# A two-layer hybrid decoder trunk on one core: twelve convolution taps of the second mixer go from TensorE to VectorE, and the first unit, the gate chain and the score levels are reordered

## The reference

```python
def token_mixer(h, ...):                       # h = rmsnorm(x): 256 x 1024
    z = h @ w_in                               # q, k 256 each; v, g 512; gr 16; ca, cb 512
    log_a = log_sigmoid(gr @ w_gate_up + b_gate) / 16
    o = gla_chunked(q / 8, k, v, log_a)        # 4 heads, gated linear attention, causal
    o = rmsnorm(o) * silu(g)
    u = ca * sigmoid(cb)                       # 512 channels
    u = causal_dwconv(u, conv_w, conv_b)       # 31 taps, each channel by itself
    u = silu(layernorm(u))                     # over the 512 channels
    return concat([o, u]) @ w_out

# layer 0: x + swiglu(h), width 2816.  layer 1: x + top-2-of-8 experts of the same width
```

## Time and profile before

| | us |
|---|---|
| median of three runs | 1210.74 |
| the profiled execution | 1210.83 |
| its span | 1209.0 |
| TensorE (PE) matmul busy | 1193.7 (99%) |
| VectorE (DVE) busy | 981.4 (81%) |
| ScalarE (ACT) busy | 795.6 (66%) |
| GpSimd (POOL) busy | 48.9 (4%) |

### The profile page before, as it was taken

How to read it: one execution, slowest core, us unless ns; L and a number is a source line. 1 busy time by engine, 2 the same in 40 slices (tenths; PEclk the granted TensorE clock), 3 DMA queues, 4 the chain that set the end, 5 groups by cost and what they waited for, 6 DMA issues and landing times.

```text
span 1209.0 us, 16770 instructions
## 1 busy us (share of the span) xinstructions
PE 1193.7 (99%) x6775; PEld 1030.6 (85%) x6775; DVE 981.4 (81%) x938; ACT 795.6 (66%) x757; POOL 48.9 (4%) x77
## 2 busy tenths in 40 slices
PE   8999999999999999999999999999999999999997
PEld 8998999999899888888888888888888888888885
DVE  5998664445669879989979879879889979979987
ACT  5976544334567657687768768668668668767764
POOL 4000000000100000000000000000000000000000
PEclk9999999999999999999999999999999999999999
DMA  9942555655545159999999999999999999999990
GB/s 273 369 139 86 192 175 178 197 183 179 204 160 190 54 189 368 380 370 392 375 374 391 376 375 389 377 376 388 381 385 375 381 386 373 381 388 375 395 341 36
DMA packets 182556, 359.61 MB, mean 297 GB/s; under 512 B 9190, under 2 KB 68940, under 8 KB 182476
## 3 DMA queue, kind: packets, MB, share of 16 engines
q1 hardware_dynamic: 178284, 343.28, 79.3%
q0 software_dynamic: 4176, 15.21, 3.3%
q10 hardware_dynamic: 16, 0.00, 0.0%
HBM read 350.60 MB, written 7.86 MB: 296 GB/s over the span
## 4 chain that ended last, share of the span: by engine, by line
PE 89%; DVE 5%; ACT 2%; issue 1%; SPq 1%; DMA 1%; ACTq 0%; DVEq 0%
PE YB L2018 18%; PE WBS L1997 13%; PE WBS L1999 13%; PE WBS L1998 13%; PE YB L1635 6%; PE WBS L1562 4%; PE WBS L1564 4%; PE WBS L1563 4%; PE YB L2009 2%; PE YB L2033 2%; PE WBS L1749 1%; DVE acc L1013 1%; PE YB L1616 1%; DVE w_lo L916 1%; DMA raw<-in_w_in 1%
## 5 line engine op out<-in xcount | busy, mean ns | idle before, releaser
L916 DVE TENSOR_TENSOR w_lo<-raw,w_hi 128x2048 fp32r<-128x2048 f32 x319 | 716.1, 2285 | 86.1 <-ACT w_hi L571 85.9
L571 ACT ACTIVATE w_hi<-raw 128x2048 fp32r<-128x2048 f32 x324 | 598.9, 1915 | 14.2 <-DMA raw<-in_w_in 10.2
L1997 PE MATMUL WBS<-w_hi,t_hi 128*128 128x512 f32 x704 | 278.7, 396 | 0.6 <-DVE w_lo L916 0.5
L1999 PE MATMUL WBS<-w_hi,t_lo 128*128 128x512 f32 x704 | 274.8, 390 | 0.0
L1998 PE MATMUL WBS<-w_lo,t_hi 128*128 128x512 f32 x704 | 274.3, 390 | 0.0
L1997 PEld LDWEIGHTS WBS<-w_hi,t_hi 128*128 128x128 f32 x704 | 132.3, 188 | 29.8 <-issue 2.9
L1999 PEld LDWEIGHTS WBS<-w_hi,t_lo 128*128 128x128 f32 x704 | 132.1, 188 | 28.2
L1998 PEld LDWEIGHTS WBS<-w_lo,t_hi 128*128 128x128 f32 x704 | 132.4, 188 | 26.3
L1562 PE MATMUL WBS<-t_hi,w_lo 128*128 128x256 f32 x448 | 127.5, 285 | 0.0
L1563 PE MATMUL WBS<-t_hi,w_hi 128*128 128x256 f32 x448 | 126.8, 283 | 0.0
L1564 PE MATMUL WBS<-t_lo,w_hi 128*128 128x256 f32 x448 | 126.8, 283 | 0.0
(11 more groups left out here) (315 smaller groups left out, 1384.3 us busy)
## 6 DMA issues: line engine op xcount, KB each, us to landing
raw<-in_we_down SPq DMA_DIRECT2D x88, 1024.0 KB, 7.0
raw<-in_we_gate SPq DMA_DIRECT2D x80, 1024.0 KB, 7.0
raw<-in_we_up SPq DMA_DIRECT2D x80, 1024.0 KB, 6.9
raw<-in_w_in SPq DMA_DIRECT2D x20, 1024.0 KB, 5.7
raw<-in_wd_gate SPq DMA_DIRECT2D x11, 1024.0 KB, 5.3
raw<-in_wd_up SPq DMA_DIRECT2D x11, 1024.0 KB, 5.4
raw<-in_wd_down SPq DMA_DIRECT2D x11, 1024.0 KB, 4.9
raw<-in_w_out SPq DMA_DIRECT2D x8, 1024.0 KB, 8.1
```

The source lines that it names most:

```text
L571: act.activation(w_hi[:, hi_slot(n, item), :], raw[slot][:], ACT.Copy).then_inc(hi_ready, 1)
L916: dve.tensor_tensor(w_lo[slot][:], raw[slot][:], w_hi[:, hi_slot(n, item), :].bitcast(F32), ALU.subtract).then_inc(lo_ready, 1)
L1997: pe.matmul(bank, xs_hi[:, k0 + k, :], hi[:, k, :], start=start, stop=False)
L1999: ins = pe.matmul(bank, xs_lo[:, k0 + k, :], hi[:, k, :], start=False, stop=stop)
```

## The change

It has four parts.

1. **First unit in halves.** SP loads the first unit of V0 as two transfers, and ScalarE and VectorE make its first half before they split the first token tile's activations. GpSimd's cast of the masks waits for the third unit's `w_hi`.
2. **Gate chain moved up**, in the first mixer alone: ScalarE does Abs, Exp and Ln ahead of units 3, 4 and 5, and VectorE's `cum` comes ahead of their `w_lo`.
3. **Levels in pairs.** TensorE does levels 0 and 1 one behind the other, and levels 2 and 3. The read-out of level 3 goes from ScalarE's eight block copies to one masked copy on VectorE. This holds for both mixers.
4. **Twelve taps.** In the second mixer the last six items of group 2 (taps 25 to 30 and, with them, 9 to 14) go from TensorE to VectorE. TensorE then has 26 items; between the levels stand 2, 2, 1, 1 and 4. VectorE's second batch of diagonal matrices has two in place of eight. VectorE adds its share to TensorE's (two new instructions), and ScalarE's copy of the second half waits for the first of these.

```diff
@@ constants @@
-        COARSE, FINE = 4, 5
-        COARSE_READS = [2, 4, 8, 16]
+        COARSE, FINE = 3, 6
+        COARSE_READS = [2, 4, 8]
+        SHARED = 6
+        PE_WORK = [PE_CONV, PE_CONV[:len(PE_CONV) - SHARED]]
+        DVE_WORK = [DVE_CONV, DVE_CONV[:42] + [(2, w) for n in range(TAPS - SHARED, TAPS) for w in (n - APART, n)] + DVE_CONV[42:]]
+        FIRST_SHARED = TAPS - SHARED - APART
@@ sync @@
+                if n == 0:
+                    dst = raw[0][:].rearrange("p (k c) -> p k c", k=k)
+                    sp.dma_start(dst[:, 0:k // 2], src[:, 0:k // 2]).then_inc(first_half_raw, 16)
+                    sp.dma_start(dst[:, k // 2:], src[:, k // 2:]).then_inc(raw_ready[0], 16)
+                    return
@@ gpsimd @@
+            pool.wait_ge(hi_ready, 3)
             step(pool.tensor_copy(masks[:], mask_f[:]))
@@ scalar, mixer @@
-                hi(b + 4)
-                hi(b + 5)
+                if l:
+                    hi(b + 4)
+                    hi(b + 5)
                 preload(ACT.Exp)
...
                 act.activation(Difs[:, 0], Difs[:, 0], ACT.Ln, bias=1.0).then_inc(gate_ln, 1)
-                hi(b + 6)
+                if l:
+                    hi(b + 6)
+                else:
+                    hi(b + 3)
+                    hi(b + 4)
+                    hi(b + 5)
...
-                coarse(3)
                 diagonals(3)
                 decays(7)
                 diagonals(7)
...
-                    for c in (2, 3):
+                    if l and r:
+                        act.wait_ge(shares_added, 1)
+                    for c in ((3,) if l else (2, 3)):
@@ scalar, start @@
             square(0, 1)
+            act.wait_ge(first_half_raw, 16)
+            act.activation(w_hi[:, hi_slot(0), 0:UNIT // 2], raw[0][:, 0:UNIT // 2], ACT.Copy).then_inc(first_half_hi, 1)
             turned(0, 0)
...
-            hi(3)
             mixer(0)
@@ vector, mixer @@
+                        if c == 2:
+                            if w == FIRST_SHARED:
+                                dve.wait_ge(cu_ready, 2 * l + 2)
+                                dve.tensor_scalar(acc[:, c, :], cu[:, c, w:w + T], ...).then_inc(conv_step[c], 1)
+                            else:
+                                dve.wait_ge(conv_step[c], shared_taps.index(w))
+                                dve.scalar_tensor_tensor(out=acc[:, c, :], ...).then_inc(conv_step[c], 1)
...
-                conv(8)
+                if l:
+                    conv(24)
+                else:
+                    lo(b + 5)
+                    conv(12)
+                    lo(b + 6)
...
-                conv(18)
+                conv(14)
...
-                conv(8)
+                level_read_out(3)
+                conv(6)
...
+                if l:
+                    dve.wait_ge(conv_step[2], 2 * SHARED)
+                    for r in (1, 0):
+                        rows = slice(64 * r, 64 * (r + 1))
+                        if r == 0:
+                            dve.wait_ge(conv_placed, 4 * l + 1)
+                        dve.tensor_tensor(acc[rows, 2, :], acc[rows, 2, :], WB[2 + r][rows, 0:T], ALU.add).then_inc(shares_added, 1)
+                    dve.wait_ge(shares_added, 2)
@@ tensor, mixer @@
                 level(0)
+                level(1)
                 pe.wait_ge(cu_ready, 2 * l + 1)
                 channels("CA1")
-                level(1)
                 channels("CB1")
-                level(2)
                 pe.wait_ge(v_ready, 2 * l + 1)
                 tokens("G0")
+                level(2)
                 level(3)
...
-                conv(3)
+                between = [2, 2, 1, 1, 4] if l else [3, 3, 3, 3, 4]
+                conv(between[0])
                 level(5)
```

More of the change, by code:

```diff
@@ L265, in trunk @@
         diag_ready, diag_used = sem("diag_ready"), sem("diag_used")
-        conv_step = [sem(f"conv_step{c}") for c in range(2)]
+        conv_step = [sem(f"conv_step{c}") for c in range(3)]
+        shares_added = sem("shares_added")
         pairs_ready, batch_ready, conv_done, conv_placed, conv_added, acc_summed = (sem(s) for s in (
@@ L683, in mixer @@
                 decays(1)
+                if l == 0:
+                    hi(b + 6)
                 hi(b + 7)
@@ L1081, in mixer @@
                 dve.tensor_copy(gr_t, YB[0:2 * RANK, 0, 0:T]).then_inc(gr_copied, 1)
-                if l == 0:
-                    lo(b + 2)
-                    lo(b + 3)
-                    lo(b + 4)
-                lo(b + 5)
+                lo(b + 5 if l else b + 2)
                 dve.wait_ge(logit_done, l + 1)
@@ L1103, in mixer @@
                 ins.then_inc(cum_ready, 1)
+                if l == 0:
+                    lo(b + 3)
                 differences(0)
                 differences(1)
-                lo(b + 6)
+                lo(b + 6 if l else b + 4)
                 conv_input(0)
                 make_pairs()
-                conv(8)
+                if l:
[4 more added lines that the diff above has]
+                    lo(b + 6)
                 decayed(0)
@@ L1211, in _ @@
             normalize(0, 1)
-            turned(0, 0)
             for half, made, ready in ((0, first_half_hi, first_half_lo), (1, hi_ready, lo_ready)):
+                if half:
+                    turned(0, 0)
                 part = slice(UNIT // 2 * half, UNIT // 2 * (half + 1))
@@ L1736, in conv @@
                 def conv(count):
-                    for c, w in PE_CONV[done[0]:done[0] + count]:
+                    for c, w in PE_WORK[l][done[0]:done[0] + count]:
                         n = done[0]
@@ L1749, in conv @@
                             ins = pe.matmul(WB[2 + r][:, T * (c - 2):T * (c - 1)], both[rows, :], cu[rows, c, w:w + T],
[L1750 removed]
+                                            start=(w == APART - 1), stop=(w == TAPS - 1 or n == len(PE_WORK[l]) - 1))
                         if n < BY_SCALAR:
                             ins.then_inc(diag_used, 1)
[L1753 removed]
+                        elif n == len(PE_WORK[l]) - 1:
                             ins.then_inc(conv_done, 1)
@@ L1835, in mixer @@
                 pe.wait_ge(v_ready, 2 * (l + 1))
-                conv(3)
+                between = [2, 2, 1, 1, 4] if l else [3, 3, 3, 3, 4]
+                conv(between[0])
                 level(5)
-                conv(3)
+                conv(between[1])
                 level(6)
-                conv(3)
+                conv(between[2])
                 level(7)
-                conv(3)
+                conv(between[3])
                 level(8)
-                conv(4)
+                conv(between[4])
                 pe.wait_ge(coarse_read, COARSE_READS[-1] * (l + 1))
```

26 lines of the change are left out of this document (15 added, 11 removed).

## The result

| | before | after |
|---|---|---|
| median of 20 runs each, us | 1210.77 (1210.29 to 1211.2) | 1212.58 (1210.47 to 1214.28) |
| ratio, 95% interval | | 1.0016, 1.0010 to 1.0022 |
| profiled execution, us | 1210.83 | 1212.21 |
| its span, us | 1209.0 | 1210.4 |
| TensorE busy, VectorE busy, us | 1193.7, 981.4 | 1191.5, 987.2 |

The change made the kernel slower by 0.16%, 1.8 us. I had forecast 1210.6 and no change. The time lies in the range given, but the direction is not the one forecast. I had taken 2.4 us for the least that a measurement can tell from no change; with 20 runs of each kernel the interval is 0.7 us to either side, and the 1.8 us stand clear of it. The runs after also lie further apart: 3.8 us, against 0.9 us before.

A forecast was written before the change was run, and what follows sets the result against it. The prediction took TensorE's work plus a few short waits as the bound. First mixer -1.8, second mixer -0.8, +1.9 and +0.6 summed to -0.1: 1210.6 us against the median, no change, range 1208.3 to 1212.6.

The forecast's parts named there:

- The start: First token tile: with the first unit in halves, TensorE's fifth k-step starts at 12.9 instead of 13.98; gain 1.0 us.
- The gate chain up: First mixer: moving it gives nothing by itself and costs nothing; unit 3 (Q) keeps 0.4 us of slack.
- The sum: First mixer as a whole: 1.0 from the start plus 0.8 from the pairs, 1.8 us gained.
- Levels in pairs: Both mixers: each pair saves one set of rounded/plain float32 switches, 0.39 us; two pairs gain 0.8 us a mixer.
- Twelve taps, up to level 4: Second mixer: shared taps in a row stand 0.5 us apart; VectorE meets level 4, 0.8 us earlier, just in time.
- From level 4 to o: Second mixer: TensorE waits for silu behind the sixteenth diagonal matrix; o starts 13.75 us after level 4, not 11.85, 1.9 later.
- Behind o: Second mixer, o to output projection: the same matmuls stand there, with the same 12 and 4 items; no cost counted.
- a late unit 3: First mixer, rival: unit 3 behind the gate chain comes late, 1212.2 us with a slip of 2.0, 1213.2 with 3.0; chance 0.10.
- The layernorm: Second mixer: VectorE's extra taps and additions make centring late, so TensorE waits 0.6 us before the squares' sum.
- Silu not last: Second mixer, rival: o waits for VectorE's last copy, 12.3 us after level 4 in place of 13.75; 1209.2 us; chance 0.22.
- the halves did bring their gain: Start of the kernel, rival denied here: the halves bring nothing, 0 in place of 1.0, so 1211.6 us; chance 0.13.

The follow-up runs named there:

- experiment 8: The kernel before with the first unit in halves alone; cast and gate chain stay: 1210.65 us, ratio 0.9998.
- Experiments 8 to 10: On the kernel before: halves alone (experiment 8), paired levels alone (1210.49 us), halves and paired levels together (1210.58 us).
- Experiment 3: The changed kernel with twelve unread 128x128 matmuls on TensorE in the wait before o of the second mixer: 1211.06 us, ratio 1.0004.
- experiment 6: The kernel of experiment 2 with the first half of unit 12's `w_lo` behind VectorE's centring in the second mixer: 1210.14 us, ratio 0.9993.
- experiment 2: The changed kernel with silu ahead of the last six diagonal matrices in the second mixer: 1209.43 us, ratio 0.9995.
- experiment 4: The changed kernel with six unread matmuls on TensorE in the wait before o of the second mixer: 1211.86 us, ratio 1.0006.
- experiment 5: The changed kernel with 3, 3, 3, 3 and 4 items between the second mixer's levels and six fewer behind o: 1209.17 us, ratio 0.9987.

## Why the prediction was wrong

**The start** was −1.0 and measured −1.44. The mechanism was right; VectorE began 0.29 sooner than the 9.18 I counted from. The cast of the masks, moved out of the way of `w_lo`, met unit 2's and took 3.08 instead of 2.04 without harm. Moving it was not needed: in experiment 8 it stays, and `w_lo` takes 1.21 all the same, because the second half is over before GpSimd comes to the cast (12.69).

**The gate chain up** I had costed at nothing, with a danger for unit 3. The danger did not come: Q starts at 32.36 without a wait, `w_lo` of unit 3 is ready at 31.5. Whether it gives "nothing by itself" was not run; but in "what the mixers gain or lose should reach the end one for one" I took the start and the pairs as gains that reach the end on their own. Experiments 8 to 10 show that they do not: without the gate chain, and with VectorE's taps where they were, 2.1 us of TensorE's time in the first mixer bring nothing. The sum came out right (−2.16 against −1.8) because the three were in the change together; that part of the forecast was luck.

**Levels in pairs**, −0.8 in each mixer: measured −0.72 and −0.72. The second pair of the second mixer, answering to the earlier trace rows; two levels start 0.95 apart and one set of switches is paid:

```profile
373.52 1.11 PE L1825 MATMUL YB<-qkE 64*128 64x64 f32 x16
374.47 1.06 PE L1825 MATMUL YB<-lnw 64*128 64x64 f32 x16
375.46 0.39 PE L1642 MATMUL WBS<-w_hi,t_hi 128*128 128x256 f32 x1
```

**Twelve taps, up to level 4.** The taps in a row stand 0.49 apart, I took 0.5 (four from 374.56 on, the next instruction at 376.52):

```profile
374.56 2.04 DVE L1038 SCALAR_TENSOR_TENSOR acc<-cu,taps,acc 128x256 f32<-128x256 f32 x4
376.52 0.69 DVE L1082 TENSOR_TENSOR qkE<-qk,Difs 128x512 f32<-128x512 f32 x1
```

Level 4 met VectorE without a wait, as forecast.

**From level 4 to o.** The instruction-by-instruction count held to a tenth: level 6's copy was put at 6.0 and came at 5.95, level 8 at 7.4 and came at 7.30, item 7 at 8.3 and came at 8.29, silu's end at 13.7 and came at 13.59, o at 13.75 and came at 13.73. The price of the table load from the trace held, too (1.28 for the load, and silu's start 1.51 behind it). One small slip: the last copy at 12.2 is 0.45 later than today's end of it (396.03 − 384.28 = 11.75), not 0.3; nothing hangs on it.

**Behind o: the step that failed.** "The same matmuls stand there up to the output projection, with the same 12 and 4 items" is true, and I took from it that they take the same 11.6 us. They took 13.23, since TensorE's granted clock fell to 0.50 behind the wait of 3.5 us, and my own forecast had put that wait there (the tenth item at 9.65, o at 13.75). I had worked out the idle time and not asked what it does to the clock. In both mixers of the kernel before the clock is at 1.00 and no gap has this length; only behind its last matmul does its trace show the clock fall. The Trainium skill (TensorE: Matmul & The Clock Gate, Why this matters for your kernels) warns against idle gaps between bursts of matmuls for this very reason; the trace of the changed kernel agrees. Experiment 3 shows the cause, with the change's order of work otherwise kept: with the gap filled the clock stays at 1.00 and the stretch takes 11.60. With this term the sum is −0.1 + 1.64, and the forecast would have been 1212.3. The median is 0.3 above that; that part I did not trace. That the time still fell inside the range is luck: the upper end, 1212.6, was there for a late unit 3, which did not come, and the median is 0.02 below it.

**The layernorm** was +0.6 and measured +0.76. Putting the half of `w_lo` behind the centring takes 0.45 of it back (experiment 6); the other 0.3 I put down to the two additions and a later second half of the mean, which no run parts.

**The rivals.** "Silu not last" did not come in the changed kernel, but experiment 2 makes it so, and gives 12.23 to o (12.3 forecast) and 1209.43 (1209.2 forecast). Unit 3 was not late and the halves did bring their gain. The rival that was missing is the one that won: an idle TensorE comes back slower.

## What to carry to other kernels

Count an idle stretch of TensorE at what it does to the clock afterwards as well as at its length: here 3.5 us of idle cost another 1.6 us in the 4 us behind them, and where the wait could not be taken away, matmuls that nobody reads in the gap brought 1.3 us back. Work taken off an engine that has nothing to put in its place gained nothing here: before moving work, look for what ends the wait of that engine now. And gains on one engine should not be added up where a second engine runs without a gap beside it; what looks worth nothing by itself, as the gate chain here, may be what lets the others through (1.3 us with it, 0.05 without it for the start in halves).

## What the runs showed of the hardware that I had not expected

- TensorE at half its clock for about 3.4 us behind an idle gap, at full clock again while it kept working: with 3.54 idle from 395.6 to 399 (changed kernel), with 1.99 from 396.5 to 400 (experiment 4), with 1.97 from 401.7 to 405 (experiment 5), with 2.06 from 394.9 to 398.3 (experiment 6). In these four the fall comes not with the first matmul but 0.2 to 1.2 us after the work resumes: in experiment 6 the first four pairs of o are at the quick rate of 0.46 and 0.39 before they go to 0.64. The gap of 0.65 (experiment 3) left it alone; the gap of 2.05 (experiment 2) did so in the profiled execution, though behind gaps of 1.97 to 2.06 in three others it fell (experiments 4, 5 and 6).
- The Trainium skill (SBUF — State Buffer, Who interferes with whom) has a VectorE instruction with two SBUF inputs and a GpSimd instruction that reads SBUF exclude each other, the first to start holding the port. The cast shows it from both sides: before, it took 2.04, its start falling into the first half of `w_lo`, and held the second half to 2.06; it took 3.08 in the changed kernel, where `w_lo` of unit 2 had started first (22.23, and kept its 2.29); and 1.04 in experiment 8, where VectorE was busy with activations that it reads partly from PSUM.
- The switch between rounded and plain float32 matmuls: 0.36 us for each isolated level (0.72 less for two pairs in a mixer); where two levels stand together only one set is paid.
